# A hybrid encoder step on one core: search steps placed by the unit's width, three masks made in the next mixer, and that mixer's units in another order

## What is computed

```python
idx_score = jnp.einsum('bqhs,bqh->bqs', jax.nn.relu(sc), wi)
idx_score = jnp.where(chunk_mask(q_pos, k_pos)[None], idx_score, -jnp.inf)
_, sel = lax.top_k(idx_score, topk)            # mixer A: the chosen keys
...
logits = einsum(qg, kg) * HEAD_DIM ** -0.5;  p = softmax(logits);  out = einsum(p, vg)   # A, over the chosen keys
logits = einsum(q_nope, k_nope) + einsum(q_rope, k_rope);  ...                           # B, over all keys
y = concatenate([out_a, out_b]) @ w_o
```

## Time and profile before

| | |
|---|---|
| median of 3 runs | 3270.11 us (3267.1 to 3271.65) |
| profiled execution | 3271.4 us, of which the span from first to last instruction is 3269.6 us |
| busy over the span | PE 2994.6 us (92%), DVE 1742.8 us (53%), ACT 1280.6 us (39%), POOL 169.4 us (5%) |
| mean granted TensorE clock | 0.955 of 2.4 GHz |
| mixer B | 326.3 to 590.9 us of the span |
| mixer A | 592.3 to 724.9 us |

### The profile page before, as it was taken

One profiled execution on the slowest core, in us unless ns is written; L12 is line 12 of the kernel. 1 busy time (PEld: TensorE's weight loads), 2 busy tenths in 40 slices (PEclk: granted clock), 3 DMA queues, 4 the chain that ended last, 5 costly groups with the idle time before them and its releaser, 6 DMA issues. The chain is left out here.

```text
span 3269.6 us, 48973 instructions
## 1 busy us (share of the span) xinstructions
PE 2994.6 (92%) x17421; PEld 2533.1 (77%) x17421; DVE 1742.8 (53%) x3767; ACT 1280.6 (39%) x2682; POOL 169.4 (5%) x240
## 2 busy tenths in 40 slices
PE   6984887799899999999989798988898999999998
PEld 5771445468899999999989566865688999999998
DVE  4438788765455444444441465148754444444545
ACT  4334787463322222222243355357533222222223
POOL 0000222330000000000000131000000000000000
PEclk9995999899999999999989799999999999999999
DMA  4110100101211111111221201120201111111112
GB/s 133 51 33 3 37 13 1 46 30 47 69 51 38 51 38 38 51 38 51 79 96 55 85 2 49 52 71 1 76 0 52 51 38 39 51 38 51 38 38 75
DMA packets 147231, 152.09 MB, mean 47 GB/s; under 512 B 18156, under 2 KB 123236, under 8 KB 147108
## 3 DMA queue, kind: packets, MB, share of 16 engines
q1 hardware_dynamic: 147108, 150.54, 15.0%
HBM read 126.75 MB, written 23.24 MB: 46 GB/s over the span
## 5 line engine op out<-in xcount | busy, mean ns | idle before, releaser
L223 PE MATMUL ffn_up<-hlow_r,ffn_uhi 128*128 128x384 f32 (+1 forms) x2112 | 691.5, 327 | 0.0
L2107 DVE SCALAR_TENSOR_TENSOR ffn_cv<-ffn_G,ffn_ctap,ffn_cv 128x256 f32<-128x256 f32 (+1 forms) x352 | 168.9, 501 | 493.0 <-ACT ffn_cv L2033 488.3
L223 PEld LDWEIGHTS ffn_up<-hlow_r,ffn_uhi 128*128 128x128 f32 x2112 | 398.3, 189 | 0.9
L2027 ACT ACTIVATE ffn_G<-ffn_up 128x384 f32<-128x384 f32 (+2 forms) x176 | 65.3, 398 | 824.0 <-PE ffn_up L224 824.0
L2140 DVE TENSOR_TENSOR xres<-ffn_dn,xres 128x512 f32<-128x512 f32 (+1 forms) x396 | 263.6, 687 | 132.5 <-PE ffn_dn L224 121.2
L222 PE MATMUL ffn_dn<-ffn_dhi,ffn_ahi 128*128 128x512 f32 x704 | 280.7, 399 | 2.9
L224 PE MATMUL ffn_dn<-ffn_dhi,ffn_alo 128*128 128x512 f32 x704 | 278.3, 395 | 0.0
L223 PE MATMUL ffn_dn<-ffn_dlo_r,ffn_ahi 128*128 128x512 f32 x704 | 278.3, 395 | 0.0
L222 PE MATMUL ffn_up<-mixed_c_r,ffn_uhi 128*128 128x384 f32 (+1 forms) x528 | 174.6, 331 | 5.9 <-DVE ulo_r L2084 5.9
L222 PE MATMUL ffn_up<-mixed_a_r,ffn_uhi 128*128 128x384 f32 (+1 forms) x528 | 174.6, 331 | 5.7 <-DVE ulo_r L2084 5.7
L222 PE MATMUL ffn_up<-mixed_b_r,ffn_uhi 128*128 128x384 f32 (+1 forms) x528 | 174.2, 330 | 0.0
(11 more groups left out here) (474 smaller groups left out, 6965.9 us busy)
## 6 DMA issues: line engine op xcount, KB each, us to landing
ulo<-in_w_up_dram SPq DMA_DIRECT2D x44, 512.0 KB, 5.0
ffn_ulo<-in_w_up_dram SPq DMA_DIRECT2D x44, 512.0 KB, 4.7
ffn_dlo<-in_w_down_dram SPq DMA_DIRECT2D x22, 1024.0 KB, 4.9
w_d<-in_w_in_odd_dram SPq DMA_DIRECT2D x7, 768.0 KB, 9.9
proj_even_x<-in_x_prompt_dram SPq DMA_DIRECT2D x8, 512.0 KB, 3.4
xres<-in_x_prompt_dram SPq DMA_DIRECT2D x8, 512.0 KB, 4.5
scratch_x<-xres SPq DMA_DIRECT2D x8, 512.0 KB, 3.5
x_d<-scratch_x SPq DMA_DIRECT2D x8, 512.0 KB, 3.9
```

What stands on the lines that cost most here:

```text
L223: nc.tensor.matmul(out, lh, rl, start=False, stop=False)
L2027: s.activation(G[:, g0:g0 + w], upbank(c, b, 0)[:, j:j + w], ACT.Copy).then_inc(g_out, 1)
L2107: last = v.scalar_tensor_tensor(cv[:, 0, j:j + w], G[:, g0 - 2 + tapno:g0 - 2 + tapno + w], ctap[:, c, tapno:tapno + 1], cv[:, 0, j:j + w] ...
```

## The change

It does five things. The counting functions `chunks`, `chunks_until` and `before_in_bank` move into a class that is given the order of the units (`halves`, unused, goes). The search steps of mixer B are placed by the width of the unit: none at tiles 0 and 8, one at tiles 1 to 5, two at tiles 6 and 7 (the first of the two stands, on DVE, ahead of the peaks, and on ACT ahead of the second group of pieces). `next_float` and `room_for_ties` move to pass 33, the masks of tiles 2 and 3 to pass 34, that of tile 4 to pass 35; none is left behind the last unit. The masks of tiles 5, 6 and 7 are made in mixer A, on DVE, at the end of its passes 4, 9 and 14. And mixer A takes its units in the order `MIXED`: the six narrow tiles (0 to 4 and 8) of pairs 0, 1, 2, then the three wide ones (5 to 7) of these pairs, then pair 3 as before.

```diff
+NARROW, WIDE = [0, 1, 2, 3, 4, NT], [5, 6, 7]
+MIXED = ([(p, t) for p in range(3) for t in NARROW] + [(p, t) for p in range(3) for t in WIDE] +
+         [(3, t) for t in range(TILES)])
...
 STEPS = 32
+TWICE, ONCE = (6, 7), (1, 2, 3, 4, 5)
+def search_steps():
+    at, done = {}, 0
+    for i, (p, t) in enumerate(ALL):
+        n = min(STEPS - done, 2 if t in TWICE else 1 if t in ONCE else 0)
+        at[i] = list(range(done, done + n))
+        done += n
...
+SEARCH_ENDS = max(i for i in SEARCH_AT if SEARCH_AT[i])
+CHOSEN_B = {SEARCH_ENDS + 2: (2, 3), SEARCH_ENDS + 3: (4,)}
+CHOSEN_A = {4: (5,), 9: (6,), 14: (7,)}
...
@@ ACT, pass i
                 if i + 1 < n_units:
                     exponential(i + 1, 1)
+                if mla and len(SEARCH_AT[i]) > 1:
+                    count_below(SEARCH_AT[i][0])
                 pieces_of(act, "act", i, "t", 1)
                 if i + 2 < n_units:
                     exponential(i + 2, 0)
-                if mla and i < STEPS:
-                    count_below(i)
+                if mla and SEARCH_AT[i]:
+                    count_below(SEARCH_AT[i][-1])
@@ DVE, peak
                 dve.wait_ge(s_ready[h], FROM + chunks_until(i))
+                if dsa and t in chosen:
+                    dve.wait_ge(told, chosen[t])
@@ DVE, pass i
                 if i + 1 < n_units:
                     over_sum(i + 1, 1)
+                if mla and len(SEARCH_AT[i]) > 1:
+                    count_below(SEARCH_AT[i][0])
                 if i + 2 < n_units:
                     for h in range(2):
                         peak(i + 2, h)
+                if mla and len(SEARCH_AT[i]) > 1:
+                    settle(SEARCH_AT[i][0])
                 if i:
                     pieces_of(dve, "dve", i, "x")
                     output(i - 1)
-                if mla and i < STEPS:
-                    count_below(i)
+                if mla and SEARCH_AT[i]:
+                    count_below(SEARCH_AT[i][-1])
                 if i + 2 < n_units:
                     over_sum(i + 2, 0)
-                if mla and i < STEPS:
-                    settle(i)
-                if mla and i == STEPS:
+                if mla and SEARCH_AT[i]:
+                    settle(SEARCH_AT[i][-1])
+                if mla and i == SEARCH_ENDS + 1:
                     next_float()
                     room_for_ties()
-                if mla and i > STEPS:
-                    select(i - STEPS - 1)
+                if mla or dsa:
+                    for t in (CHOSEN_B if mla else CHOSEN_A).get(i, ()):
+                        select(t)
             output(n_units - 1)
-            if mla:
-                for j in range(n_units - STEPS - 1, n_top):
-                    select(j)
```

More of the change, by code:

```diff
@@ L822, with __init__, chunks, chunks_until @@
 ALL = [(p, t) for p in range(PAIRS) for t in range(TILES)]
+NARROW, WIDE = [0, 1, 2, 3, 4, NT], [5, 6, 7]
+MIXED = ([(p, t) for p in range(3) for t in NARROW] + [(p, t) for p in range(3) for t in WIDE] +
+         [(3, t) for t in range(TILES)])
 EXPAND = {1: [0, 1], 2: [2], 3: [3], 4: [4], 5: [5], 6: [6], 7: [7], 8: [8]}
[L826 to L848, removed]
+class Units:
+    def __init__(self, order):
+        self.order = order
+    def chunks(self, i):
+        w = key_tile(self.order[i][1])[0]
+        return [(0, 0, 512), (1, 512, w - 512)] if w > 512 else [(i % 2, 0, w)]
+    def chunks_until(self, i):
+        return sum(len(self.chunks(j)) for j in range(i + 1))
+    def before_in_bank(self, i, half):
+        for j in range(i - 1, -1, -1):
+            for c, (x, _, _) in enumerate(self.chunks(j)):
+                if x == half:
+                    return j, self.chunks_until(j - 1) + c + 1
+        return None
 TPB = 3
 STEPS = 32
+TWICE, ONCE = (6, 7), (1, 2, 3, 4, 5)
[5 more added lines that the diff above has]
+        done += n
+    assert done == STEPS
+    return at
+SEARCH_AT = search_steps()
+SEARCH_ENDS = max(i for i in SEARCH_AT if SEARCH_AT[i])
+CHOSEN_B = {SEARCH_ENDS + 2: (2, 3), SEARCH_ENDS + 3: (4,)}
+CHOSEN_A = {4: (5,), 9: (6,), 14: (7,)}
 class Groups:
-    def __init__(self, copier, expands):
+    def __init__(self, order, copier, expands):
         self.of = []
@@ L863, in __init__ @@
         self.jobs = {}
-        for i, (p, t) in enumerate(ALL):
+        for i, (p, t) in enumerate(order):
             here = [("t", h, g) for g in range(2) for h in range(2) if blocks(t, g)]
@@ L894, in attention @@
     mask = None if dsa else consts[{"b": "mask_chunk", "c": "mask_causal", "d": "mask_strict"}[kind]]
-    n_units = len(ALL)
+    units = Units(MIXED if dsa else ALL)
+    order, chunks, chunks_until = units.order, units.chunks, units.chunks_until
+    n_units = len(order)
     def copier(what, x, j):
@@ L1040, in scores @@
             def scores(i, c):
-                p, t = ALL[i]
+                p, t = order[i]
                 k0 = key_tile(t)[1]
@@ L1044, in scores @@
                 half, c0, cw = chunks(i)[c]
-                before = before_in_bank(i, half)
+                before = units.before_in_bank(i, half)
                 if before is not None:
@@ L1086, in piece @@
             def piece(i, x, what, a, j):
-                n = queries(ALL[i][1])
+                n = queries(order[i][1])
                 tp = TP[x % TPB]
@@ L1096, in piece @@
                     pe.wait_ge(prob_ready[a], FROM + i + 1)
-                    for b, r in blocks(ALL[i][1], j):
+                    for b, r in blocks(order[i][1], j):
                         last = tt.transpose(tp[0:r, (b % 4) * P:(b % 4) * P + n],
@@ L1166, in copy_piece @@
             else:
-                t, s = ALL[i][1], i % 2
+                t, s = order[i][1], i % 2
                 n, bl = queries(t), blocks(t, j)
@@ L1352, in room_for_ties, with select @@
                 dve.wait_ge(told, FROM + 8)
[L1354 to L1357 removed]
+            def select(t):
+                j, n = SEARCHED.index(t), key_tile(t)[0]
+                w = work[t][:]
                 out = src["bias"][:, src["bias_at"][t]:src["bias_at"][t] + n]
                 bar = top["bits"][:, j:j + 1].bitcast(F32)
[L1360 to L1362 removed]
+                tied, left_over = tie[:, 0:n], beyond[:, 0:n]
+                before = FROM + (8 if mla else 0) + 5 * len(chosen)
+                chosen[t] = before + 5
+                dve.wait_ge(told, before)
                 v_.tensor_scalar(tied, w, bar, -TIE, ALU.is_equal, ALU.mult).then_inc(told, 1)
[L1364 to L1365 removed]
+                v_.tensor_scalar(out, w, bar, -TIE, ALU.is_lt, ALU.mult).then_inc(told, 1)
+                dve.wait_ge(told, before + 1)
                 v_.tensor_tensor_scan(left_over, tied, tied, spare[:, j:j + 1], ALU.add, ALU.bypass).then_inc(told, 1)
[L1367 removed]
+                dve.wait_ge(told, before + 3)
                 v_.scalar_tensor_tensor(left_over, left_over, 0.0, tied, ALU.is_lt, ALU.mult).then_inc(told, 1)
[L1369 to L1370 removed]
+                dve.wait_ge(told, before + 4)
+                v_.tensor_tensor(out, left_over, out, ALU.add).then_inc(told, 1)
             if stick:
```

25 lines of the change are left out of this document (15 added, 10 removed).

## The result

The kernel after takes 3274.58 us, the median of 20 runs (3270.19 to 3276.36), against 3268.84 of the kernel before, also over 20 runs (3266.02 to 3271.65). The ratio is 1.0017, with an interval of 1.0011 to 1.0023: 5.7 us slower, within 0.2%. The forecast was 17.6 us slower. One execution of run 2 and one of run 6 took two to four times as long as all others (13100 and 6758 us); the ratios leave them out.

What follows compares the result with a forecast made beforehand. Mixer B was taken as bound by DVE and ACT, mixer A by PE. B -1.9 (start -0.8, boundaries +9.6, end -10.7) and A +19.5 gave +17.6 us: median 3287.7, its own range 3279 to 3297, 8 in 10 3270 to 3300.

Steps and rivals of the forecast that it cites:

- Three boundaries: 3 x 3.2 = 9.6 us: Mixer B, where two pairs meet: moving steps from tiles 8 and 0 to 6 and 7 loses 3.2 us each.
- A boundary is then 1.6 + 0.7: Mixer B: wide stretches cost 5.7, narrow gain 4.1, waits for DVE's verdict add 0.7; a boundary is 2.3 us dearer.
- I add 0.9 a boundary: Mixer B: PE idling in double passes brings the half clock into units PE bounds, 0.9 us (between 0 and 3).
- B's start: Mixer B, unit (0, 0): its step goes, and 0.8 of its 3.67 us is gained (bounds 0 and 3.67).
- B's end: After tile 4's output in pair 3: 25.5 us against 36.25, 10.7 gained (bounds 9.5 and 11.5).
- Three masks in A: Masks of tiles 5, 6, 7 outlast PE's one pass of cover: 13.5 us idle plus 6.0 of clock, +19.5.
- The other order by itself costs nothing: Mixer A's new unit order is free in the sum; 2 us if narrow units no longer cover hand-overs.
- The clock rule: PE runs at 2.4 GHz only while kept busy, else 1.2; without this rule the sum would be 9 us less.
- A hides the masks: Rival, mixer A passes 4, 9, 14: DVE slack makes the three masks cost nothing; 3268 us, chance 0.17.
- The boundaries cost nothing: Rival, mixer B: DVE's sum is unchanged, so boundaries are free and B gains 11.5; 3278 us, chance 0.12.
- The clock costs more: Rival: slow clock costs 3.4 us behind each mask and 2.4 at each boundary; 3296 us, chance 0.08.
- POOL is held up: Rival, mixer A: POOL's scaling slows beside masks, 3 x 0.88 = 2.6 us; 3290 us, chance 0.05.

Runs made afterwards that it cites:

- run 2: Kernel before with steps placed by width and A in order `MIXED`, masks of tiles 5, 6, 7 behind B's last unit: 3271.21 us, ratio 1.0009.
- run 6: Kernel after, with ACT copying its expanded key pieces ahead of the pass's last count in mixer B: 3270.13 us, ratio 1.0004.
- second pair of traces: Kernel before and kernel after, each profiled once more unchanged: 3269.07 and 3273.61 us.
- run 8: Kernel after with A's mask operations one to a pass and ACT's key copies ahead of its count: 3251.48 us, ratio 0.9955.
- runs 6 and 7: ACT's key copies ahead of its count, in the kernel after (3270.13 us) and in the kernel before (3263.89 against 3268.01, ratio 0.9988).
- run 3: The kernel of run 2 once more, for its trace (A in order `MIXED`, no mask in A): 3269.91 us, one execution.
- run 4: Kernel after, with the five operations of each mask in A spread over five passes, one to a pass: 3256.78 us, ratio 0.9966.
- run 5: Kernel after, with each of A's three masks made twice in a row: 3291.44 us, ratio 1.0069.

## Why the prediction was wrong, step by step

**The step that failed** is "Three boundaries: 3 x 3.2 = 9.6 us". All the seven stretches from tile 5's output to tile 2's together changed by −1.9, −0.1 and +0.4 us at the three boundaries in the first pair of traces, and by −0.3, −0.1 and −0.3 in the second. Three boundaries gained 1.5 or 0.7 us, where 9.6 were to be lost. These 10 to 11 us are nearly all of what the forecast for B missed besides its start. Its parts:

- "A boundary is then 1.6 + 0.7": the double passes grew by 2.5 and 3.0 (tile 5's and 6's, first boundary; 4.8 to 5.6 in all six), less than the 5.7 + 0.7 of the forecast, and the narrow stretches (tiles 8 and 0) gave back 4.4 to 5.4, more than 4.1. DVE's verdict on the first step hardly stands in ACT's way: in the two double passes of the first boundary ACT waits for it once, 0.25 us, where I had 0.7. By these terms alone the three boundaries come to +1.6 in the first pair of traces (tiles 5, 6, 7, 8, 0) and to −1.1 in the second.
- "I add 0.9 a boundary" for the clock had the wrong sign. The slow clock did come: 389.83 to 396.66 us has a granted clock of 0.50. But it lies in tile 6's stretch, where ACT is busy all 9.72 us. Before, it lay over PE's scores in tiles 0 and 1 (6.80 us with PE busy 6.45). In run 8, with whole clock, tile 6's stretch is 8.67, against 9.02 to 9.81 in the kernel after; by that the slow clock in it costs 0.4 to 1.1 us, an estimate, since run 8 also has ACT's copies first. Where the slow clock fell into tile 1's stretch in the kernel after (9.05 against 6.21), it cost 2.8.
- Tile 1's and 2's stretches were taken as unchanged. In the first pair of traces they gave 3.1 us over the three boundaries, in the second they lost 0.4; so this part hangs on the one trace, and the step fails without it. The 3.90 wait for ACT's key copy, from which I priced the clock, was 1.90 in the second trace. It was still the place to ask what ACT had in its queue ahead of the copy: in runs 6 and 7, with the copy first, 4.1 to 4.4 us of the whole program go.

**B's start**, −0.8 forecast within bounds of 0 and 3.67, gained 3.2 us in tile 1's stretch (8.62 to 5.44; in the second pair of traces, to 5.30). The queue's part was right: DVE's peak comes 1.0 us earlier. What the term lacked is the clock behind the wait: 1.7 us in the scores alone. (In the second pair B up to its first output is 1.9 us longer after than before, 27.49 against 25.63, with a granted clock of 0.71 instead of 0.77; in the first pair it is not.)

**B's end** was right: 10.7 us gained, 10.7 forecast; 25.5 us long, 25.5 forecast.

**Three masks in A** was right, and for the reason given. Forecast 13.5 of idle time and 6.0 of clock; measured against the kernel of run 3, 12.8 and 6.4. The three standstills are 3.32, 3.92 and 5.85 (forecast 3.9, 3.9, 4.8): PE was busy 2.97 and 2.13 in the second and third, where I had taken 3.75 and 3.35 for its cover. "Released by POOL" holds for two of the three. "The other order by itself costs nothing" was off by 1.5 us, within the 2 allowed. In all +20.8 against +19.5.

**The clock rule.** The rows of A have granted clocks of 0.50 to 0.66, 1.2 GHz for all or most of the time, in stretches that come after standstills, and 1.00 where there are none (run 4). By the Trainium skill ("TensorE: Matmul & The Clock Gate", Part 1) the engine keeps 2.4 GHz only while it is kept busy; these rows agree. But run 5, with longer standstills, has PE busy for only 0.9 us more, so the clock's price did not grow with them.

**The rivals.** "A hides the masks" falls with the three standstills and with the 1 to 1 price of run 5; it becomes true when the masks come in single operations. "The boundaries cost nothing" is the one that came true: it had 0.12, and 3278 with 0.8 for the start; with the 2.4 us more that tile 1's stretch gave there, it is 3276. The forecast itself had 0.58. "The clock costs more" was right in none of its places. "POOL is held up": POOL is busy 53.87 in A instead of 51.84, but PE's idle time, 12.8 us, is no larger than the 13.5 forecast without it.

What is left open is why, in the first pair of traces, the slow clock fell into the double passes in the kernel after and into tiles 0 and 1 before. PE idles 1.9 and 2.7 us in the two double passes of the first boundary; in the first trace after it begins 1.9 us into tile 6's stretch, in the second 0.5, and no run here held all else equal. That B gained 12.9 us in one pair of traces and 15.6 in the other is 1.9 ahead of the first output, where the granted clock differed too, and 0.8 at the boundaries.

## What to carry to other kernels

Before long work is laid onto an engine "with slack" beside a pipeline, compare the length of one uninterrupted piece, not its share of busy time, with what the bound engine still has queued: 15.2 us in three pieces cost 19.3, and in fifteen pieces 2.7. When an engine near the bound waits for a copy, look at what stands ahead of that copy in its queue before pricing any other part: moving two lines gave 4 us in either kernel. A stretch whose length hangs on where the slow clock falls is read from two traces before a term is taken from it, or a difference in it is put down to the change.

## What was not expected of the hardware

- The slow clock falls at other places in two executions of the same kernel. In the kernel before, tile 1's stretch of pair 1 is 10.04 us in one trace and 6.13 in the other; the sum over tiles 0 and 1 differs by 3.1 us, and the whole program's time by 2.3 (3271.4 and 3269.07). The Trainium skill ("TensorE: Matmul & The Clock Gate", Part 1) tells that the slow matmuls at a kernel's start differ from run to run; here it is so in the middle of one.
- The price of the slow clock did not grow with the standstill: with 15.2 us more of it in run 5, the mean clock of A fell to 0.88, and the same matmuls kept PE busy 135.00 us instead of 134.12.
- POOL's scalings take longer beside the spread mask operations: busy 62.47 us in A in run 4, 53.87 with whole masks, 51.84 without any, for the same 72 instructions. The Trainium skill ("SBUF — State Buffer", Who interferes with whom) has DVE's two-port operations, and those with two inputs in SBUF, contend with GpSimd; these rows agree, as does a scaling of 64x320 that took 1.96 us beside a scan in run 4, and 0.52 in run 3. What it costs wasn't measured by itself: PE waits for POOL 3.8 us in all of A in run 4, and 2.7 in run 3.
